# Both key tiles per chunk of x, and the fronts, rotary steps and low parts of a two-block attention kernel placed anew

## The reference

```python
x = x + swa_sink_mixer(rms_norm(x, swa_norm), ...)   # 32 query heads, 4 key/value heads of 64, window of 128
h = concat([meta (16 tokens), x])
u = rms_norm_2(h, norm_w); proj = u @ w_in           # 8 stick-breaking heads of 128, 8 differential heads of 2 x 64
# differential heads: q and k normed, partial rope on 16 of 64, softmax, p0 - lam * p1
# stick-breaking heads: a = exp(log_beta + tail), tail = reversed sum of log_keep over later keys
mixed = concat([sb_o * silu(sb_g), df_o * silu(df_g)])
return (h + mixed @ w_out)[:, 16:]
```

## Time and profile before

| | us |
|---|---|
| median of 3 runs (1795.81 to 1796.63) | 1796.47 |
| the profiled execution | 1796.16 |
| its span in the trace | 1794.5 |
| PE, matmul busy | 1756.3 |
| DVE busy | 1065.3 |
| ACT busy | 911.8 |
| POOL busy | 54.2 |

### The profile page before, as it was taken

One profiled execution on the slowest core, in us unless ns is written; L12 is line 12 of the kernel. 1 busy time (PEld: TensorE's weight loads), 2 busy tenths in 40 slices (PEclk: granted clock), 3 DMA queues, 4 the chain that ended last, 5 costly groups with the idle time before them and its releaser, 6 DMA issues.

```text
span 1794.5 us, 28922 instructions
## 1 busy us (share of the span) xinstructions
PE 1756.3 (98%) x10281; PEld 1525.1 (85%) x10281; DVE 1065.3 (59%) x2443; ACT 911.8 (51%) x2010; POOL 54.2 (3%) x81
## 2 busy tenths in 40 slices
PE   6999999999999999999999999999999999999899
PEld 5788888888877888898898988889888898877899
DVE  5566667676675334564655556455564655666776
ACT  4466656666574224444545445454544545454343
POOL 1100000000001000000000000000000000000000
PEclk9999999999999999999999999999999999999999
DMA  6433333333325444322322323222222222223551
GB/s 192 130 93 99 102 97 100 100 95 92 103 80 135 137 140 129 103 83 61 95 78 69 90 52 91 82 73 82 71 83 83 63 80 74 83 83 94 157 167 54
DMA packets 283942, 173.85 MB, mean 97 GB/s; under 512 B 16176, under 2 KB 272368, under 8 KB 283840
## 3 DMA queue, kind: packets, MB, share of 16 engines
q1 hardware_dynamic: 267136, 151.08, 28.7%
q0 software_dynamic: 15632, 20.56, 5.0%
q10 hardware_dynamic: 1088, 1.08, 0.3%
HBM read 156.86 MB, written 14.66 MB: 96 GB/s over the span
## 4 chain that ended last, share of the span: by engine, by line
PE 80%; DVE 7%; ACT 5%; issue 3%; ACTq 2%; DMA 1%; SPq 0%; DVEq 0%
PE G L644 62%; PE G L940 6%; ACTq L1512 2%; PE S L1027 1%; ACT wh L1192 1%; PE O L1045 1%; PE S L940 1%; DVE wl L1745 1%; DMA raw<-in_swa_w_in 1%; PE G L756 1%; PE S L746 1%; PE G L770 1%; PE S L745 1%; PE G L731 1%; ACT chain_rs L1502 1%
## 5 line engine op out<-in xcount | busy, mean ns | idle before, releaser
L644 PE MATMUL G<-xh,wh 128*128 128x512 f32 (+1 forms) x2432 | 791.8, 360 | 3.4 <-DVE xl L1762 1.5
L644 PE MATMUL G<-xl,wh 128*128 128x512 f32 (+1 forms) x2432 | 765.4, 349 | 0.0
L644 PE MATMUL G<-xh,wl 128*128 128x512 f32 (+1 forms) x2432 | 762.9, 348 | 0.0
L644 PEld LDWEIGHTS G<-xh,wh 128*128 128x128 f32 x2432 | 426.4, 189 | 64.6 <-issue 4.8
L644 PEld LDWEIGHTS G<-xh,wl 128*128 128x128 f32 x2432 | 423.7, 188 | 60.9
L1745 DVE TENSOR_TENSOR wl<-raw,wh 128x512 fp32r<-128x512 f32 x472 | 319.5, 688 | 253.7 <-ACT wh L1192 251.3
L644 PEld LDWEIGHTS G<-xl,wh 128*128 128x128 f32 x2432 | 423.8, 188 | 51.1 <-issue 2.6
L1192 ACT ACTIVATE wh<-raw 128x512 fp32r<-128x512 f32 x472 | 283.4, 619 | 15.3 <-issue 7.7
L1569 ACT ACTIVATE att<-att,st 128x144 f32<-128x144 f32 (+3 forms) x64 | 36.9, 577 | 119.2 <-DVE wmeta L2202 68.6
L1295 ACT ACTIVATE p<-S,rq 128x256 f32<-128x256 f32 (+1 forms) x128 | 50.3, 445 | 44.6 <-PE S L746 43.1
L1305 ACT ACTIVATE p<-p,st 128x257 f32<-128x257 f32 (+1 forms) x128 | 60.5, 481 | 0.0
(11 more groups left out here) (319 smaller groups left out, 2313.3 us busy)
## 6 DMA issues: line engine op xcount, KB each, us to landing
raw<-in_w_in SPq DMA_DIRECT2D x112, 512.0 KB, 4.0
raw<-in_swa_w_in SPq DMA_DIRECT2D x68, 512.0 KB, 8.8
raw<-in_swa_w_out SPq DMA_DIRECT2D x32, 512.0 KB, 4.4
raw<-in_w_in POOLq DMA_DIRECT2D x8, 1024.0 KB, 8.1
raw<-in_w_out SPq DMA_DIRECT2D x6, 1024.0 KB, 6.8
spare<-in_w_out SPq DMA_DIRECT2D x6, 1024.0 KB, 6.7
rel_rows<-mixed POOLq DMA_DIRECT2D x16, 383.0 KB, 19.5
mixed<-in_x SPq DMA_DIRECT2D x4, 1024.0 KB, 13.4
```

The lines of the kernel that those rows point to most:

```text
L644: mm = pe.matmul(d, w[:, slot, k, :], v[:, k, a:b], start=(first and n == 0), stop=(last and n == 2))
```

## The change

In words: (1) the first key tile and the second run together, chunk by chunk, as x arrives (`key_tiles`); the row sums stand behind chunks 9 and 12, the value tile's weight quarters behind chunks 13 and 14 and later, and the key norms move to points of the two value tiles. The value weights' loads wait for less. (2) In the last unit's gate tile, each chunk stands behind the step of its point, not ahead of it. (3) Both fronts place chunks 8 to 14 and the weight quarters by tables of their own. (4) In the cumulative sum, this key tile's matmuls go before those over later key tiles. (5) The rotary moves from point 7 to point 6. (6) In the second output's front, the last gate's operations on ACT move from n = 5 to n = 10, and DVE's from step 24 to 27. (7) Before the fast pairs, three low parts of T go ahead of the first four weight quarters. (8) The first half of the first pair's weights is loaded four quarters sooner.

```diff
-        QUARTER_AT = {0: 0, 3: 1, 7: 2, 10: 3}
+        QUARTER_AT1 = {0: 0, 4: 1, 7: 2, 10: 3}
+        CHUNK_AT1 = {2: (8,), 4: (9,), 5: (10, 11), 7: (12,), 8: (13, 14)}
+        QUARTER_AT2 = {0: 0, 3: 1, 7: 2, 11: 3}
+        CHUNK_AT2 = {1: (8,), 3: (9,), 5: (10,), 7: (11,), 9: (12, 13), 11: (14,)}
...
             def value_weights(g):
-                sp.wait_ge(w_lo, 4 + 2 * (g - 1))
+                sp.wait_ge(w_lo, 4 * (g - 1))
...
-                    sp.wait_ge(w_lo, 4 * T_FAST + (14 * (j - 1) if j else 0))
                     for i in range(2):
+                        sp.wait_ge(w_lo, 4 * T_FAST + (14 * (j - 1) if j else 4 * i - 4))
...
+            def key_tiles():
+                for k in range(KC):
+                    next_chunk(k)
+                    for g in range(KV // 2):
+                        if k % QTR == 0:
+                            pe.wait_ge(w_lo, 2 * (k // QTR) + g + 1)
+                        product([G[:, g, :]], g, k, PLAIN, k == 0, k == KC - 1, keys_done if g else None)
...
-            for g in range(KV):
+            key_tiles()
+            for g in range(KV // 2, KV):
                 def at_point(p, g=g):
-                    if g == 1 and p == 3:
+                    if g == KV // 2 and p == 0:
                         first_factors()
-                    if 0 < g <= KV // 2 and p == 5:
-                        key_stat(g - 1)
+                    if g == KV // 2 and p in (3, 7):
+                        key_stat(p // 4)
                     if g > KV // 2 and p == 5:
                         value_transpose(g - 1)
-                if g == 1:
-                    pe.wait_ge(x_lo, KC)
-                gemm(T_KV + g, g % 2, [G[:, g, :]], PLAIN, at_point, next_chunk if g == 0 else None)
+                if g == KV - 1:
+                    pe.wait_ge(kv_act, 2)
+                gemm(T_KV + g, g % 2, [G[:, g, :]], PLAIN, at_point)
```

The cumulative sum on PE:

```diff
+                    for part in (lk_h, lk_l):
+                        mm = pe.matmul(z, exact[0:size, 2, 0:size], part[0:size, 0:TOK - q], start=False,
+                                       stop=n == 0 and part is lk_l, skip_group_check=True)
                     if n:
                         after(pe, b_ll, 4 * h + n)
                         q_last = sb_tile(n - 1)[2]
                         for part in (later_h, later_l):
-                            pe.matmul(S[:, n % 2, q_last - q:TOK - q], exact[:, 3, :], part[:, q_last:TOK], start=False,
-                                      stop=False, skip_group_check=True)
-                    for part in (lk_h, lk_l):
-                        mm = pe.matmul(z, exact[0:size, 2, 0:size], part[0:size, 0:TOK - q], start=False,
-                                       stop=part is lk_l, skip_group_check=True)
+                            mm = pe.matmul(S[:, n % 2, q_last - q:TOK - q], exact[:, 3, :], part[:, q_last:TOK], start=False,
+                                           stop=part is later_l, skip_group_check=True)
```

ACT, in the opening and after it (DVE has the same places, with rows 2 and 3, and its low parts of the value weights behind each of ACT's quarters):

```diff
             for quarter in range(4):
                 key_split_weights(0, quarter)
+                key_split_weights(1, quarter)
...
                     x_hi_of(c)
-            key_split_weights(1, 0)
-            key_split_weights(1, 1)
-            row_sum(0)
...
+                    if c == 9:
+                        act.wait_ge(x_in[3], 32)
+                        row_sum(0)
+                    if c == 12:
+                        act.wait_ge(sq_act, 1)
+                        row_sum(1)
+                    if c == 13:
+                        first_value_split(0)
...
+                        first_value_split(1)
+            first_value_split(2)
+            act.wait_ge(first_mm, 2)
             A(rs1[:, :], O[:, :], ACT.Copy).then_inc(rs1_ok, 1)
+            first_value_split(3)
...
-            for g in range(1, KV):
+            for g in range(KV // 2, KV):
                 for m in range(POINTS):
-                    if m == 4 and g <= KV // 2:
-                        key_square(g - 1)
-                    if m == 6 and g <= KV // 2:
-                        key_rstd(g - 1)
+                    if g == KV // 2 and m in (2, 6):
+                        key_square(m // 4)
+                    if (g, m) in ((KV // 2, 4), (KV - 1, 0)):
+                        key_rstd(g - KV // 2)
                     if m % 2 == 0:
                         split((g + 1) // 2, (g + 1) % 2, m // 2, kv_loaded(g + 1))
-                    if m == 7:
-                        key_split(g - 1) if g <= KV // 2 else value_high(0)
+                    if (g, m) in ((KV // 2, 5), (KV - 1, 1)):
+                        key_split(g - KV // 2)
+                    if g == KV - 1 and m == 6:
+                        value_high(0)
...
                 for m in range(8):
-                    if u == 4 * UNITS - 1 and m >= 8 - AHEAD:
-                        out1_chunk(m - 8 + AHEAD)
                     swa_step(u, g, m)
                     if m % 2 == 0:
                         split(T_UNIT // 2 + u + 1, 0, m // 2, unit_loaded(u + 1, 0))
+                    if u == 4 * UNITS - 1 and m >= 8 - AHEAD:
+                        out1_chunk(m - 8 + AHEAD)
...
-                    if n == 5:
+                    if n == 10:
                         finish(N2 - 1, len(TILES2) - 1, 0)
```

DVE:

```diff
+                    if (g, m) == (KV // 2, 1):
+                        kv_evict(0)
+                    if (g, m) == (KV // 2, 5):
+                        key_finish(0)
+                        kv_evict(1)
+                        key_split(0)
+                    if (g, m) == (KV - 1, 1):
+                        key_finish(1)
+                        kv_evict(2)
+                        key_split(1)
...
-                    if p == 7:
+                    if p == 6:
                         after(dve, n_rot, 64 * count)
...
-                        if m == 24:
+                        if m == 27:
                             finish(N2 - 1, len(TILES2) - 1, 2)
...
             t_low(0)
             y_add(2, 1, 0)
-            for e in range(4):
-                fast_split(e)
             t_low(1)
             t_low(2)
             t_low(3)
+            for e in range(4):
+                fast_split(e)
             y_add(3, 1, 1)
```

More of the change, by code:

```diff
@@ L1192, in split, with first_value_split @@
                 A(wh[:, slot, q, :], raw[:, slot, q, :], ACT.Copy).then_inc(w_hi, 1)
+            def first_value_split(quarter):
+                if quarter == 0:
+                    act.wait_ge(raw_in[0], 16)
+                if quarter < 3:
+                    act.wait_ge(keys_done, QTR * quarter + QTR)
+                else:
+                    act.wait_ge(tile_done, 1)
+                q = slice(QTR * quarter, QTR * quarter + QTR)
+                A(wh[:, 0, q, :], raw[:, 0, q, :], ACT.Copy).then_inc(w_hi, 1)
             def row_sum(t):
@@ L1397, in out1_front @@
                         swa_step(4 * UNITS - 1, 3, SWA_REST[n])
-                    if n in QUARTER_AT:
-                        split(T_OUT1 // 2, 1, QUARTER_AT[n], out_loaded(OUT1_LOADS, 0, 1))
-                    if n + AHEAD < KC - 1:
-                        out1_chunk(n + AHEAD)
+                    if n in QUARTER_AT1:
+                        split(T_OUT1 // 2, 1, QUARTER_AT1[n], out_loaded(OUT1_LOADS, 0, 1))
+                    for c in CHUNK_AT1.get(n, ()):
+                        out1_chunk(c)
                 act.wait_ge(tile_done, T_OUT1)
@@ L1670, in out2_front @@
                             sb_step(N2 - 1, m)
-                    if n == 5:
+                    if n == 10:
                         finish(N2 - 1, len(TILES2) - 1, 0)
-                    if n in QUARTER_AT:
-                        split(T_OUT2 // 2, 1, QUARTER_AT[n], out_loaded(OUT2_LOADS, 0, 1))
-                    if n + AHEAD < KC - 1:
-                        out2_chunk(n + AHEAD)
+                    if n in QUARTER_AT2:
+                        split(T_OUT2 // 2, 1, QUARTER_AT2[n], out_loaded(OUT2_LOADS, 0, 1))
+                    for c in CHUNK_AT2.get(n, ()):
+                        out2_chunk(c)
                 act.wait_ge(b_out, N2)
@@ L1775, in _ @@
                 key_split_weights(0, quarter)
+                key_split_weights(1, quarter)
                 for c in range(4 * quarter, 4 * quarter + 4):
                     x_lo_of(c)
-            key_split_weights(1, 0)
-            key_split_weights(1, 1)
-            row_sum(2)
-            key_split_weights(1, 2)
-            dve.wait_ge(sq_dve, 1)
-            row_sum(3)
-            key_split_weights(1, 3)
+                    if c == 9:
+                        dve.wait_ge(x_in[3], 32)
+                        row_sum(2)
+                    if c == 12:
+                        dve.wait_ge(sq_dve, 1)
+                        row_sum(3)
+                    if c == 13:
+                        split(1, 0, 0)
             dve.wait_ge(rs_done, 2)
@@ L1787, in _ @@
```

(23 more changed lines are left out.)

45 lines of the change are left out of this document (18 added, 27 removed).

## The result

The changed kernel takes 1788.07 us (median of 5 runs, 1786.97 to 1789.13) against 1796.63 for the kernel before (5 runs, 1795.81 to 1798.36): a ratio of 0.995, interval 0.994 to 0.9961, or 8.6 us. 1787.6 was forecast. The sum came out within half a us; several of its terms did not, and the experiments turned up more time than the change had brought.

The account below looks back on a forecast made before the run. PE, busy 98% of the span, bounds the kernel, so gains are its waits removed or filled. Terms -0.6 - 1.0 - 1.2 + 0.4 - 0.4 - 6.1 = -8.9 us give 1787.6 us for the median; range 1783.5 to 1791.0.

Parts of the forecast that it names:

- Opening: Start, key and value tiles: 0.7 us of waiting filled, 1.0 us wait gone, new 1.1 us wait: -0.6 us.
- Window 15 and the first front: Last attention window, first output tile: four pieces, -0.3 + 1.1 - 1.1 - 0.7 = -1.0 us, ends 0 and -2.5.
- Cumulative sums: Stick-breaking sums: keep parts first, so two matmuls hide the wait for `later_l`: -1.2 us.
- L992 keeps its wait: Heads, dfk rotary and the weight quarter: their order on DVE changes, not the time, so PE's wait at L992 stays.
- Rotary at point 6: Heads: in head 0 the quarter now stands behind the DMA landing DVE already waited for, +0.4 us.
- The third rival: Heads 1 to 7: rotary at point 6 stops DVE, PE waits 7 times 2 us, 1801.6 us; chance 0.04.
- Second front: Last head, second output tile: late gate saves 1.9 us, costs 0.5 and 1.0: -0.4 us, ends +0.6 and -1.5.
- Fast pairs: Before the six fast pairs: low parts fill DVE's idle time, part 4 starts 6.1 us sooner; ends -7.3 and -4.5.
- the first rival: Fast pairs: x for the second output lands 3 us late, -3.1 instead of -6.1, 1790.6 us; chance 0.12.

Follow-up runs that it names:

- the chunk 7 kernel: The changed kernel with chunk 7 of the first output moved behind the first weight quarter of its second tile, on ScalarE and VectorE: 1785.56 us.

## Why the prediction came out right

**Opening, -0.6.** Right in its parts: the 1.0 us for the row factors went, the new wait at L706 was 1.1 us and disappeared when the square went ahead of the copies. The traces' mean is nearer to -1.0, but single ones differ by more than that.

**Window 15 and the first front, -1.0.** Measured -1.9 in the table and -1.8 in the mean of the traces, inside its ends. Each of the four pieces was there; the grown wait came to 2.3 us (forecast 1.1 + 1.1), and the idle times alone make -0.9; the other 0.9 or so lies in gaps of PE around those waits that the view does not count as waiting.

**Cumulative sums, -1.2.** Failed; the runs show 0 over the heads. The step was "hidden by two matmuls", read as time off the path. It stood beside the statement that L992 keeps its wait, and the two contradict each other: a stretch that ends in a wait for a chain which starts ahead of the saving keeps its length. The wait at its end grows by what was saved. The price was off too: a listed wait of 0.17 us was worth 0.35 where it counted.

**Rotary at point 6, +0.4 in head 0, else 0.** The mechanism held, the size did not: head 0 lost 1.1, since to the 0.7 at its value transposes came 0.4 at the statistic of dfk, which had no term. One reading under it was wrong. It takes the rotary of head 0 as standing "directly on the landing" before. In the kernel before DVE did not wait for the landing in any head. It came from a weight quarter, which ACT's DMA issues had held up:

```profile
757.01 0.69 DVE L1745 TENSOR_TENSOR wl<-raw,wh 128x512 fp32r<-128x512 f32 x1 [3.88 <-ACT wh L1192]
```

The 1.4 us from the last issue's end to the landing, read off there, holds in head 3 of the changed kernel (from 1067.5 to 1068.9 us for dfq). In its head 0 it was 2.6 us for dfk (753.1 to 755.6), with a wait of DVE of 4.6 us:

```profile
755.66 0.71 DVE L2137 TENSOR_TENSOR chain_sq<-chain_rs,rope 128x528 f32<-128x528 f32 x1 [4.63 <-DMA chain_rs<-dfk]
```

Heads 1 to 7 lost nothing, rather 0.3 won. The third rival did not come. By the Trainium skill (DMA: Bandwidth & Descriptors, Rules for kernel authors) a DMA's semaphore is waited for late; DVE did stand for the landing here, 3.4 us for each of the two rotaries of a head, and it cost nothing in heads 1 to 7, since what stood behind it was not wanted sooner. What did count was that the eviction stands behind the rotary, in both kernels.

**Second front, -0.4.** Measured -0.6, by the mechanism of the working, with both sizes off and one term missing. At the front's 26th chunk product of 32 PE is 2.05 us ahead of the kernel before (30.51 against 32.56 us from the front's start; forecast 1.9 - 0.5). Then the wait for `xl` of chunk 7 and the longer one for `y_col` take 1.4 back (forecast 1.0). The missing term is the table: without it chunk 7 is on time and the front 0.8 us shorter. So what the late gate is worth hangs on the table. Beside the new table it brings nothing (37.39 against 37.26 us). With the old table, the late gate and the new order of the sums together bring 1.4 us (36.63 against 38.02). How the 1.4 divides between these two stays open, for both traces that have the late gate with the old order of the sums have a lower granted clock in this very stretch. Whether their longer waits brought that clock about, two traces cannot tell.

**Fast pairs, -6.1.** The mechanism and the size held: -6.05 with that edit alone. In the changed kernel it was -5.4: the second wait at L952 took 1.1 us there and 0.4 with the edit alone (its line is L940 there). The late operation was a DMA: DVE stood 0.59 us for x of the second output.

```profile
1666.53 0.42 DVE L2423 TENSOR_TENSOR chain_rs<-G,chain_sq 128x256 f32<-128x256 f32 x1 [0.59 <-DMA chain_sq<-x]
```

SP had issued it at 1657.52, behind 2 MB of weights. That is the first rival, at a fifth of its price. In the other kernels this wait was 0.4 to 0.7 us.

So the total was right partly by luck: the sums failed by 1.2 us, head 0 and the fast pairs by 0.7 each, and the first front gave 0.8 more, the opening 0.4, the seven heads 0.3 and the second front 0.2. These are read from traces, which give 8.0 us in all, where the medians give 8.6.

## What to carry to other kernels

Before a small wait is costed as gain, look at the next long wait on the same engine and at where the chain that ends it begins: if it begins ahead of the small wait, nothing is won until that chain is shortened. Where it does count, a short wait between matmuls can cost more than the view lists, so measure from start to start. An overwriting operation needs to wait for the last reader of its buffer and not for the end of the task that the buffer belonged to; here this one dependency, one us a head, was worth about as much as the whole change. And an edit that is worth nothing now should be tried again once the pace is set elsewhere.

## What the runs showed of the hardware

A wait of PE can cost more than its length. In the 5.4 us without work the granted clock fell, and it was 0.50 to 0.59 until nearly 1670 us; this cost 1.7 us on top of the 4.3 saved. The 2.3 us wait at 528 us is the same in the traces of the changed kernel and of the one with the old order of the sums, with a granted clock of 1.00 after it in the first and 0.92 and 0.74 in the second, where the front took 1.6 us longer. So a wait of this length is sometimes followed by the lower clock and sometimes not. It may be a part of the spread among the runs of one kernel, but not all of it: with the rotary back at point 7 the slowest run (1788.92 us) has the lowest mean clock, 0.996, and the fastest (1784.12) has 1.000, while in the chunk 7 kernel the slowest (1787.25) has 1.000. The lower clock is also where PE's 3.5 us less of busy time come from in part: at the lower clock the same instructions are busy longer.
